# The p\*v matmuls of sliding-window attention, issued by key block first instead of by head half first, in a one-core hybrid encoder layer

## Chip, cores and metric

The kernel runs on one core of a Trainium2 chip. The metric is the device time of one execution in microseconds (us); for the kernel before, the median of three runs is 2016.85.

## What is computed

One layer of a streaming encoder, for 1024 frames of a new stream and 32 frames of a running one, model width 1024, all in float32. After a conditioning vector has scaled and shifted the input, one wide projection gives queries, keys and values of two branches and their gates. Branch A is sliding-window attention (16 query heads, 2 key/value heads, head width 64), branch B an mLSTM matrix memory; both are projected, gated, merged and normalised, and a convolutional feed-forward part follows. The change is in branch A alone. Its core in the reference:

```python
def banded_attention(qb, kb, vb, qpos, kpos, sinks):
    s = jnp.einsum('nbqhgd,nbshd->nbhgqs', qb.astype(jnp.float32), kb.astype(jnp.float32)) * (HEAD_DIM_A ** -0.5)
...
    s = s - slopes[None, None, :, :, None, None] * dist[None, :, None, None]
    s = jnp.where(visible[None, :, None, None], s, -jnp.inf)
...
    mx = jnp.maximum(jnp.max(s, -1, keepdims=True), sink)
    p = jnp.exp(s - mx)
    p = p / (jnp.sum(p, -1, keepdims=True) + jnp.exp(sink - mx))
    o = jnp.einsum('nbhgqs,nbshd->nbqhgd', p, vb.astype(jnp.float32))
    return o.astype(qb.dtype)
```

A chunk of 64 queries sees the keys of its own and the two chunks before, at most 192; the running stream's 32 queries see 128 cached keys and their own 32.

## The kernel before

Every engine has a program of its own, written out by hand, and semaphores tie them. Features lie on the partitions, positions on the free dimension. A weight panel (128 output columns of a projection) comes by DMA, POOL splits it into a high and a low part (L365, L367), and TensorE runs three matmuls for each of 8 input blocks and each third of the positions (gemm_half, L400): a whole panel is six "half panels" of 12 matmuls.

Attention runs interleaved with the panels of the other branch. For each of the 17 chunks (16 of the new stream, 1 of the running one) and each of the two key/value groups there is what is called a unit here, a = 2c + g, so 34 units, 0 to 33. On TensorE a unit goes through three steps with a half panel behind each, and the units overlap in a pipeline (att_chunk, L488): scores of unit a+1, half panel, transposes of unit a, half panel, p\*v of unit a, half panel.

- att_scores (L454): q times k for four head pairs into px banks 0 and 1, L463; for g = 0 also the transposes of v, L460 and L461.
- VectorE adds the ALiBi term and takes the maximum (att_max, L1247), ScalarE takes the exponential (att_exp, L834), VectorE normalises (att_norm, L1272, the product at L1278).
- att_transpose (L467): the probabilities are turned, block of older keys to bank 2 (L472), own chunk to bank 3 (L473); ScalarE copies them to pta (L844) and ptb (L845).
- att_values (L476): p\*v. The output is bank 4, partitions 0 to 63 for the even head of each pair (e = 0) and 64 to 127 for the odd one (e = 1), 256 columns (4 pairs of 64 queries). For each e, the first matmul takes the older keys (rows w - kb: 128 from chunk 2 on, 64 in chunk 1, none in chunk 0; L482), the second the own chunk (kb = 64 rows, 32 for the running stream; L484), accumulated. A weight operand is 64 columns of v, so an instruction fills 64 columns of the array.
- att_take (L1281, the copy at L1285): VectorE moves bank 4 to SBUF. It comes in VectorE's order between att_max and att_norm of the next unit.

The wait for pt_rdy and o_used stands ahead of the first p\*v matmul, the last one raises pv_rdy, for which att_take and the next copy to pta wait. VectorE has other work at two places of attention: behind chunk 3 it prepares rows of mLSTM gates (L1305 to L1311), behind chunk 15 it scans them (L1317 to L1323), each time before att_max of the next chunk.

Of the kernel before, what the change touches and what calls it, by code (L numbers as in the profile page):

```python
# [27 lines left out]
CH = 64  # L28
# [102 lines left out]
def wait(eng, sem, v):  # L131

    if isinstance(v, int) and v <= 0:
        return
    eng.wait_ge(sem, v)


def build(nc, io):
    ctx = ExitStack()
    with ctx:  # L140
# [18 lines left out]
        def after(name, shape, dt=F32):  # L159
            return at(name, shape, (place["end"] + 31) // 32 * 32, dt)  # L160
# [30 lines left out]
        vt = after("v_tok", [P, 2, 2, P])  # L191
        pb = after("probs", [P, 2, 4, BAND])
        pta = after("probs_ta", [P, 4, P])
        ptb = after("probs_tb", [P, 4, P])
# [56 lines left out]
        px = ctx.enter_context(nc.psum_tensor("px", [P, 5, 512], F32))  # L251
# [54 lines left out]
        def weights(p):  # L306
            return wo[:, p - WO_PANELS[0], :, :] if p in WO_PANELS else wt[:, p - TAIL_PANELS[0], :, :] if p in TAIL_PANELS else whl[:, SLOT[p], :, :]
# [81 lines left out]
        def _(pe):  # L389
            mm = nc.tensor.matmul  # L390
# [21 lines left out]
            for m in range(KT + 4):  # L412
                if 1 <= m <= KT:
                    pe.wait_ge(ada_row, m)
                    wait(pe, ada_mod, m - 1)
                    for i in range(2):
                        last = nc.tensor.transpose(px[:, 4, 2 * i:2 * i + 2], mrow[:, (m - 1) % 2, i * P:(i + 1) * P],
                                                   ident[0:2, 0:2])
                    last.then_inc(ada_col, 1)
                if m < KT:  # L420
                    for i in range(2):
                        q = 2 * m + i
                        pe.wait_ge(ada_in[q % KT], (q // KT + 1) * 16)
                        for k in range(KT):
                            last = mm(px[0:2, 3, i * P:(i + 1) * P], silu[:, 1, k, :], ada[:, q % KT, k * P:(k + 1) * P],  # L425
                                      start=(k == 0), stop=(k == KT - 1))
                        last.then_inc(ada_used, 1)
                for p in range(2):
# [7 lines left out]
                    for j, (wi, xi) in enumerate(((0, 0), (0, 1), (1, 0))):  # L436
                        for n in range(NT):
                            last = mm((acc, px)[p][:, n, 0:NW], whl[:, p, wi, k * P:(k + 1) * P],
                                      XA[:, xi, k, n * NW:(n + 1) * NW], start=(k == 0 and j == 0),
                                      stop=(k == KT - 1 and j == 2))  # L440
# [35 lines left out]
            def att_values(a, par, g, w, kb):  # L476
                pe.wait_ge(pt_rdy, a + 1)
                wait(pe, o_used, a)
                for e in range(2):
                    out = px[64 * e:64 * e + 64, 4, 0:4 * CH]  # L480
                    if w > kb:
                        mm(out, vt[0:w - kb, par, 0, g * 64:g * 64 + 64], pta[0:w - kb, :, 64 * e:64 * e + 64],  # L482
                           start=True, stop=False)
                    last = mm(out, vt[0:kb, par, 1, g * 64:g * 64 + 64], ptb[0:kb, :, 64 * e:64 * e + 64],  # L484
                              start=(w == kb), stop=True)
                last.then_inc(pv_rdy, 1)

            def att_chunk(c, par, w, kb, wp, kbp):  # L488

                slot = SLOT[P_ATT + c]  # L490
                first = isinstance(c, int) and c == 0
                for g in range(2):
                    if first and g == 0:
                        for half in range(2):
                            gemm_half(P_ATT, slot, 0, half, XA)
                        att_scores(0, 0, 0, 0, w, kb)
                        gemm_half(P_ATT, slot, 1, 0, XA)
                        continue
                    before = (c * 2 - 1, 1 - par, 1, wp, kbp) if g == 0 else (c * 2, par, 0, w, kb)
                    att_scores(c, c * 2 + g, par, g, w, kb)  # L500
                    gemm_half(c + P_ATT, slot, *divmod(3 * g, 2), XA)
                    att_transpose(before[0], before[2], before[3], before[4])
                    gemm_half(c + P_ATT, slot, *divmod(3 * g + 1, 2), XA)
                    att_values(*before)
                    gemm_half(c + P_ATT, slot, *divmod(3 * g + 2, 2), XA)
# [8 lines left out]
            att_chunk(NCH, 0, WIN + TS, TS, BAND, CH)  # L514
            att_transpose(2 * NCH + 1, 1, WIN + TS, TS)
            att_values(2 * NCH + 1, 0, 1, WIN + TS, TS)


# [8 lines left out]
            for h in range(HB):  # L527
                last = mm(px[:, 0, 128 + 9 * h:137 + 9 * h], sel[:, h, :], mprow[:, :], start=True, stop=True)
# [175 lines left out]
            w = weights(P_OUT)  # L704
            for k in range(KT):
                pe.wait_ge(mg_lo, k + 1)
                for j, (wi, xi) in enumerate(((0, 0), (0, 1), (1, 0))):
                    for n in range(NT):
                        last = mm(first[n], w[:, wi, k * P:(k + 1) * P], XA[:, xi, k, n * NW:(n + 1) * NW],
                                  start=(k == 0 and j == 0), stop=(k == KT - 1 and j == 2))  # L710
# [1017 lines left out]
```

## Time and profile before

| | |
|---|---|
| median of 3 runs | 2016.85 us (2012.32 to 2017.06) |
| profiled execution, its time | 2017.29 us |
| its span | 2015.5 us |
| TensorE busy (PE) | 1947.1 us, 97% |
| weight loads (PEld) | 1847.2 us, 92% |
| VectorE (DVE) / ScalarE (ACT) / POOL | 52% / 31% / 27% |
| mean granted clock of TensorE | 0.986 |

A row of the timeline has a start and a time in us from the start of the span, the engine, the line, the operation, "output<-inputs" and shapes. For a matmul "128\*64" is the part of the array in use, rows by columns, and "128x256" the moving operand; a float32 matmul instruction leaves two records, so "x2" is one instruction. Brackets at the end hold the engine's idle time before the row and what released it. Neighbouring records of one kind are merged into one row. How fast matmuls run is read from their starts, since a record's end is modelled and overlaps its neighbour.

### The profile page before, as it was taken

How to read it: one execution, taken by the hardware profiler on the slowest of the kernel's cores; microseconds unless marked ns; L12 is line 12 of the kernel's file. 1: busy time of each engine (PE TensorE's matmuls, PEld its weight loads, DVE VectorE, ACT ScalarE, POOL GpSimd, SP SyncE). 2: the span in 40 equal slices, each digit the busy share in tenths (PEclk: the TensorE clock that was granted, in tenths of full speed). 3: DMA queues.
4: the chain of work that ended last, by engine and by line, in shares of the span. 5: the costliest groups of instructions: out<-in, count | busy, mean ns of one | idle time of the engine just before them, and what ended most of it. 6: DMA issues, size and time to landing. Idle time of an engine off the chain costs nothing.

```text
span 2015.5 us, 29507 instructions
## 1 busy us (share of the span) xinstructions
PE 1947.1 (97%) x11919; PEld 1847.2 (92%) x11919; DVE 1045.8 (52%) x1885; ACT 621.3 (31%) x1409; POOL 553.4 (27%) x312
## 2 busy tenths in 40 slices
PE   8889999999999999999899999999999999999995
PEld 6889888888799999988899998999999999999995
DVE  2796454434543333454434487754454455535488
ACT  1102543445222232334311136322222223222333
POOL 2332212111122222212233624432323323233230
PEclk9999999999999999999999999999999999999997
DMA  7562111111222333324634300111111111111102
GB/s 309 200 200 97 66 43 59 48 43 64 76 85 96 109 124 99 115 69 163 206 105 158 112 20 2 62 53 43 42 53 43 53 42 43 53 43 52 43 30 79
DMA packets 74184, 171.40 MB, mean 85 GB/s; under 512 B 8496, under 2 KB 37680, under 8 KB 73920
## 3 DMA queue, kind: packets, MB, share of 16 engines
q1 hardware_dynamic: 27168, 91.50, 13.3%
q10 hardware_dynamic: 46880, 78.02, 11.6%
q8 instruction: 94, 1.54, 0.3%
q14 instruction: 42, 0.34, 0.1%
HBM read 137.27 MB, written 32.22 MB: 84 GB/s over the span
## 4 chain that ended last, share of the span: by engine, by line
PE 85%; DVE 9%; ACT 2%; DVEq 1%; issue 1%; ACTq 1%; DMA 1%; POOL 0%; POOLq 0%
PE acc L400 30%; PE px L670 15%; PE acc L670 9%; PE px L680 7%; PE acc L680 4%; DVE adaT_tmp L1222 4%; PE px L647 2%; PE px L463 2%; PE px L484 2%; PE px L482 2%; PE px L425 2%; PE acc L647 1%; PE px L564 1%; PE px L566 1%; PE px L565 1%
## 5 line engine op out<-in xcount | busy, mean ns | idle before, releaser
L400 PE MATMUL acc<-x_hilo_a,w_hilo 128*128 128x352 f32 x4176 | 730.7, 330 | 20.8 <-ACT x_c L780 9.9
L400 PEld LDWEIGHTS acc<-x_hilo_a,w_hilo 128*128 128x128 f32 x4176 | 677.5, 191 | 39.8 <-issue 29.1
L365 POOL CAST w_hilo<-w_raw 128x1024 fp32r<-128x1024 f32 x133 | 144.3, 1085 | 1296.5 <-PE acc L400 790.2
L367 POOL TENSOR_TENSOR w_hilo<-w_raw,w_hilo 128x1024 fp32r<-128x1024 f32 x133 | 342.3, 2574 | 10.6
L670 PE MATMUL px<-x_hilo_a,w_hilo 128*128 128x352 f32 x1968 | 319.2, 322 | 0.0
L670 PEld LDWEIGHTS px<-x_hilo_a,w_hilo 128*128 128x128 f32 x1968 | 315.4, 189 | 0.5 <-issue 0.5
L670 PE MATMUL acc<-x_hilo_a,w_hilo 128*128 128x352 f32 x1200 | 194.2, 321 | 0.0
L670 PEld LDWEIGHTS acc<-x_hilo_a,w_hilo 128*128 128x128 f32 x1200 | 191.4, 188 | 0.0
L680 PE MATMUL px<-ffn_act,w_hilo 128*128 128x352 f32 x864 | 146.2, 324 | 0.0
L680 PEld LDWEIGHTS px<-ffn_act,w_hilo 128*128 128x128 f32 x864 | 140.3, 189 | 0.2
L1100 ACT ACTIVATE u_rows<-px,ffn_consts 128x352 f32<-128x352 f32 (+2 forms) x110 | 49.5, 478 | 238.6 <-PE px L670 238.6
L1546 DVE SCALAR_TENSOR_TENSOR x_c<-px,mod,x_c 128x352 f32<-128x352 f32 (+2 forms) x181 | 80.4, 483 | 64.4 <-PE px L680 64.4
L1517 DVE COPY conv_out<-u_rows 128x2 f32<-128x2 f32 x44 | 17.3, 394 | 171.5 <-ACTq L1105 171.4
L1520 DVE SCALAR_TENSOR_TENSOR stage<-u_rows,ffn_consts,stage 128x1058 f32<-128x1058 f32 x44 | 88.9, 2021 | 21.5 <-ACT stage L1107 21.5
L1222 DVE CUSTOM_DVE_ANT_0 adaT_tmp<-adaT_ring,silu_bc 128x1024 f32<-128x1024 f32 x64 | 94.1, 1507 | 5.1 <-issue 4.2
L849 ACT ACTIVATE stage<-acc 128x352 f32<-128x352 f32 x123 | 54.9, 457 | 130.7 <-PE acc L400 114.1
L680 PE MATMUL acc<-ffn_act,w_hilo 128*128 128x352 f32 x504 | 87.6, 324 | 2.6 <-POOL w_hilo L367 1.5
L680 PEld LDWEIGHTS acc<-ffn_act,w_hilo 128*128 128x128 f32 x504 | 81.8, 189 | 3.3 <-issue 3.1
L1100 ACT ACTIVATE u_rows<-acc,ffn_consts 128x352 f32<-128x352 f32 (+2 forms) x66 | 30.2, 482 | 164.8 <-PE acc L670 164.8
L400 PE MATMUL acc<-x_hilo_b,w_hilo 128*128 128x352 f32 x504 | 80.5, 322 | 0.5 <-DVE stage L1439 0.5
L400 PEld LDWEIGHTS acc<-x_hilo_b,w_hilo 128*128 128x128 f32 x504 | 80.3, 188 | 0.7 <-issue 0.7
L1546 DVE SCALAR_TENSOR_TENSOR x_c<-acc,mod,x_c 128x352 f32<-128x352 f32 (+2 forms) x107 | 48.4, 487 | 56.8 <-PE acc L680 56.8
(231 smaller groups left out, 2318.9 us busy)
## 6 DMA issues: line engine op xcount, KB each, us to landing
w_raw<-in_w_panels SPq DMA_DIRECT2D x142, 512.0 KB, 3.7
z_spill<-stage ACTq DMA_DIRECT2D x41, 528.0 KB, 2.6
adaT_ring<-in_w_adaT ACTq DMA_DIRECT2D x32, 512.0 KB, 4.2
stage<-z_spill ACTq DMA_DIRECT2D x20, 528.0 KB, 4.8
ada_ring<-in_w_ada SPq DMA_DIRECT2D x16, 512.0 KB, 9.4
zc<-z_spill ACTq DMA_DIRECT2D x8, 1024.0 KB, 7.5
x_c<-in_x SPq DMA_DIRECT2D x8, 528.0 KB, 10.1
x_c<-in_x ACTq DMA_DIRECT2D x8, 528.0 KB, 3.8
```

What stands on the lines that cost most here:

```text
L365: nc.gpsimd.tensor_copy(to[:, 0, :], raw[:, s, :]).then_inc(w_hi, 1)
L367: nc.gpsimd.tensor_tensor(to[:, 1, :], raw[:, s, :], to[:, 0, :].bitcast(F32), ALU.subtract).then_inc(w_ready, 1)
L400: last = mm(acc[:, n, 0:NW], whl[:, slot, wi, k * P:(k + 1) * P], rhs[:, xi, k, n * NW:(n + 1) * NW], start=(k == 0 and j == 0), stop=(k = ...
L425: last = mm(px[0:2, 3, i * P:(i + 1) * P], silu[:, 1, k, :], ada[:, q % KT, k * P:(k + 1) * P], start=(k == 0), stop=(k == KT - 1))
L647: last = mm(to, w[:, wi, k * P:(k + 1) * P], XA[:, xi, k, n * NW:(n + 1) * NW], start=(k == 0 and j == 0), stop=(k == KT - 1 and j == 2))
L670: last = mm(to, w[:, wi, k * P:(k + 1) * P], XA[:, xi, k, n * NW:(n + 1) * NW], start=(k == 0 and q == 0), stop=(k == KT - 1 and q == 2))
L680: done = mm(to, w[:, wi, col:col + P], act[:, xi, k, n * NW:(n + 1) * NW], start=(first and k == 0 and q == 0), stop=(last and k == 1 and ...
L849: A(ST[:, slot, n * NW:(n + 1) * NW], acc[:, n, 0:NW], ACT.Copy).then_inc(acc_free[n], 1)
L1100: last = A(ub[:, i, 2 + a + 2 * s:2 + b + 2 * s], src[:, a - n * NW:b - n * NW], ACT.Identity, bias=fc[:, j, i, 0:1])
L1222: V.tensor_tensor_reduce(adaT_tmp[:, s, :], adaT[:, i, :], sbc[:, s, :], 1.0, 0.0, ALU.mult, ALU.add, ast[:, i, s:s + 1])
L1520: V.scalar_tensor_tensor(ST[:, i, 0:CW], ub[:, i, 0:CW], fc[:, j, i, 1:2], ST[:, i, 0:CW], ALU.mult, ALU.add)
L1546: last = V.scalar_tensor_tensor(XC[:, m, a:b], src[:, a - n * NW:b - n * NW], mod[:, 5, m, s:s + 1], XC[:, m, a:b], ALU.mult, ALU.add)
```

## The change

The loop over the two halves e is turned inside out: first the older-key block for both halves, then the own chunk for both. Each output half is accumulated as before, in the same order of its two terms. skip_group_check only tells the build that two accumulations are open at once. Nothing else is changed.

```diff
--- before.py
+++ after.py
@@ -476,13 +476,14 @@
             def att_values(a, par, g, w, kb):
                 pe.wait_ge(pt_rdy, a + 1)
                 wait(pe, o_used, a)
+                outs = [px[64 * e:64 * e + 64, 4, 0:4 * CH] for e in range(2)]
+                if w > kb:
+                    for e in range(2):
+                        mm(outs[e], vt[0:w - kb, par, 0, g * 64:g * 64 + 64], pta[0:w - kb, :, 64 * e:64 * e + 64],
+                           start=True, stop=False, skip_group_check=True)
                 for e in range(2):
-                    out = px[64 * e:64 * e + 64, 4, 0:4 * CH]
-                    if w > kb:
-                        mm(out, vt[0:w - kb, par, 0, g * 64:g * 64 + 64], pta[0:w - kb, :, 64 * e:64 * e + 64],
-                           start=True, stop=False)
-                    last = mm(out, vt[0:kb, par, 1, g * 64:g * 64 + 64], ptb[0:kb, :, 64 * e:64 * e + 64],
-                              start=(w == kb), stop=True)
+                    last = mm(outs[e], vt[0:kb, par, 1, g * 64:g * 64 + 64], ptb[0:kb, :, 64 * e:64 * e + 64],
+                              start=(w == kb), stop=True, skip_group_check=True)
                 last.then_inc(pv_rdy, 1)
 
             def att_chunk(c, par, w, kb, wp, kbp):
```

On TensorE the p\*v step of a unit with 128 older keys, with the neighbouring rows ("x2" here is two instructions that read alike; lines with - are those of before, with + those of the change; L400 is the half panel, L460 the first transpose of the next unit):

```order
 L400 MATMUL acc<-x_hilo_a,w_hilo 128x352 x11
 L482 MATMUL px<-probs_ta,v_tok 64x256 [waits o_used,pt_rdy]
-L484 MATMUL px<-probs_tb,v_tok 64x256
-L482 MATMUL px<-probs_ta,v_tok 64x256
-L484 MATMUL px<-probs_tb,v_tok 64x256
+L482 MATMUL px<-probs_ta,v_tok 64x256
+L485 MATMUL px<-probs_tb,v_tok 64x256 x2
 L400 MATMUL acc<-x_hilo_a,w_hilo 128x352 x12
 L460 MATMUL px<-ident,v_stage 128x128 [waits s_used,st_rdy]
```

The first instruction with its waits stays, the two L482 now stand together and the two own-chunk ones behind them.

The second place is behind chunk 15, TensorE's side in the changed kernel, from the half panel ahead of the p\*v of unit 31 to the scores of unit 33 (the last of the running stream's two):

```order
L400 MATMUL acc<-x_hilo_a,w_hilo 128x352 x12
L482 MATMUL px<-probs_ta,v_tok 64x256 [waits o_used,pt_rdy]
L482 MATMUL px<-probs_ta,v_tok 64x256
L485 MATMUL px<-probs_tb,v_tok 64x256 x2
L400 MATMUL acc<-x_hilo_a,w_hilo 128x352 [waits acc_free1]
L400 MATMUL acc<-x_hilo_a,w_hilo 128x352 x11
L463 MATMUL px<-k_stage,q_stage 128x160 [waits s_used]
L463 MATMUL px<-k_stage,q_stage 128x160 x3
```

Between this p\*v step and the scores that wait for s_used lies one half panel, as before; only the two middle p\*v matmuls have changed places.

The third is VectorE's side of the same place in the changed kernel, from the take of unit 30 to the first row of unit 32 (line numbers are one higher than before):

```order
L1286 COPY x_c<-px 128x4x64 [waits pv_rdy]
L1275 TENSOR_TENSOR row_den<-row_sum,exp_sink 128x4 [waits ex_rdy]
L1277 RECIPROCAL row_den<-row_den 128x4
L1279 TENSOR_TENSOR probs<-probs,row_den 128x768
L1318 TENSOR_TENSOR rowC<-rowC,rowD 4x1056 [waits row_a]
L1320 TENSOR_TENSOR stage<-stage,rowC 4x1056
L1322 SCALAR_TENSOR_TENSOR rowD<-rowE,stage 4x1056
L1323 SCALAR_TENSOR_TENSOR rowM<-stage 4x1024
L1324 SCALAR_TENSOR_TENSOR rowM<-stage,small 4x32
L1253 TENSOR_TENSOR probs<-px,alibi 128x2x160 [waits tr_rdy,s_rdy]
```

Nothing moved here. The gate rows stand between the normalising of unit 31 and the row that takes up the scores of unit 32.

## Rows read from the trace of the kernel before

**Rows 1.** page of the profile: span, TensorE's busy time, chain by line
```profile
span 2015.5 us, 29507 instructions
PE 1947.1 (97%) x11919; PEld 1847.2 (92%) x11919; DVE 1045.8 (52%) x1885; ACT 621.3 (31%) x1409; POOL 553.4 (27%) x312
PE acc L400 30%; PE px L670 15%; PE acc L670 9%; PE px L680 7%; PE acc L680 4%; DVE adaT_tmp L1222 4%; PE px L647 2%; PE px L463 2%; PE px L484 2%; PE px L482 2%; PE px L425 2%; PE acc L647 1%; PE px L564 1%; PE px L566 1%; PE px L565 1%
```
**Rows 2.** windows, the attention stretch: busy by engine, PEclk, DMA share, GB/s
```profile
190.00:560.00 370.00, 365.18 (x2156) 307.06 (x2155) 161.86 (x396) 158.12 (x509) 64.75 (x36) 1.00 0.16 57
```
**Rows 3.** waits of TensorE, 190 to 700: in total, times, longest
```profile
PE px L472 <- DVE probs L1278: 1.6, 1, 1.6
PE px L463 <- DVEq L1260: 0.7, 1, 0.7
```
**Rows 4.** timeline, V(10) on TensorE: start us, us, engine line operation
```profile
300.23 0.65 PE L482 MATMUL px<-probs_ta,v_tok 128*64 128x256 f32 x2
300.81 0.64 PE L484 MATMUL px<-probs_tb,v_tok 64*64 64x256 f32 x2
301.38 0.65 PE L482 MATMUL px<-probs_ta,v_tok 128*64 128x256 f32 x2
302.53 0.43 PE L400 MATMUL acc<-x_hilo_a,w_hilo 128*128 128x352 f32 x1
```
**Rows 5.** groups by line and form, L482: busy us, mean ns
```profile
L482 PE MATMUL px<-probs_ta,v_tok 128*64 128x256 f32 x120 | 38.7, 405 | 1.3 <-ACT probs_tb L845 1.3
L482 PE MATMUL px<-probs_ta,v_tok 64*64 64x256 f32 x8 | 1.3, 402 | 0.0
```
**Rows 6.** timeline, V(0) in chunk 0, matmuls and weight loads
```profile
202.02 0.65 PE L484 MATMUL px<-probs_tb,v_tok 64*64 64x256 f32 x4
202.02 0.20 PEld L484 LDWEIGHTS px<-probs_tb,v_tok 64*64 64x64 f32 x4 [0.22 <-issue]
202.60 0.43 PE L400 MATMUL acc<-x_hilo_a,w_hilo 128*128 128x352 f32 x1
```
**Rows 7.** timeline, V(2) in chunk 1, TensorE
```profile
218.42 0.66 PE L482 MATMUL px<-probs_ta,v_tok 64*64 64x256 f32 x4
219.44 0.43 PE L400 MATMUL acc<-x_hilo_a,w_hilo 128*128 128x352 f32 x1
```
**Rows 8.** timeline, unit 11: normalise, transpose, copy, p*v
```profile
303.45 0.96 DVE L1278 TENSOR_TENSOR probs<-probs,row_den 128x768 f32<-128x768 f32 x1
308.01 0.27 PE L472 MATMUL px<-ident,probs 128*128 128x128 f32 x1
309.58 0.58 ACT L845 ACTIVATE probs_tb<-px 64x512 f32<-64x512 f32 x1
310.90 0.65 PE L482 MATMUL px<-probs_ta,v_tok 128*64 128x256 f32 x2
```
**Rows 9.** timeline, behind chunk 3: take, normalise of unit 8, its transposes
```profile
260.43 0.42 DVE L1285 COPY x_c<-px 128x256 f32<-128x256 f32 x1 [4.20 <-PE px L484]
274.84 0.96 DVE L1278 TENSOR_TENSOR probs<-probs,row_den 128x768 f32<-128x768 f32 x1
276.25 0.27 PE L472 MATMUL px<-ident,probs 128*128 128x128 f32 x1
```
**Rows 10.** timeline, behind chunk 15: take, scan, scores and transposes that wait
```profile
513.63 0.42 DVE L1285 COPY x_c<-px 128x256 f32<-128x256 f32 x1 [3.84 <-PE px L484]
518.84 4.39 DVE L1321 TENSOR_TENSOR_SCAN rowD<-rowE,stage 4x1056 f32<-4x1056 f32 x1
526.84 1.35 PE L463 MATMUL px<-k_stage,q_stage 128*128 128x160 f32 x8 [0.68 <-DVEq L1260]
531.70 0.33 PE L472 MATMUL px<-ident,probs 128*128 128x128 f32 x1 [1.60 <-DVE probs L1278]
```
**Rows 11.** windows, two stretches at the end of attention (columns of rows 2)
```profile
540.00:543.40 3.40, 2.14 (x8) 0.75 (x8) 1.72 (x1) 1.06 (x2) 3.32 (x2) 1.00 0.41 164
543.40:547.00 3.60, 3.60 (x14) 3.38 (x13) 1.43 (x6) 0.00 (x0) 0.52 (x1) 0.53 0.52 151
```

## Prediction

> **What bounds the kernel now.** I read the page first. TensorE is busy for 97% of the span and the chain that ended last is nearly all TensorE, the p\*v lines L482 and L484 with 2% each in it [rows 1]. A busy TensorE can still contain time in which it streams nothing, so the share alone does not say what an edit of its work is worth; I went on to the attention stretch. There, of 370 us, TensorE is busy for 365.18 at full granted clock, while VectorE and ScalarE are busy for less than half [rows 2]. The waits of TensorE in and after it are single ones, the longest of a kind 1.6 us [rows 3]. So what attention takes is what TensorE's own instructions take one after another, and time cut there comes off the end, as long as nothing else is late.
>
> Then the timeline of one p\*v step. I call a chunk and key/value group a unit (34 of them, 0 to 33, two to a chunk) and its rows between two half panels V(a). V(10) starts at 300.23 and the half panel behind it at 302.53 [rows 4]: 2.30 us for four matmul instructions, each of them two passes in the trace ("x2"). The four start 0.57 to 0.58 us apart. Every neighbour has another height: 128\*64, 64\*64, 128\*64, 64\*64. The boundary at 300.81 keeps the column half and the one at 301.38 changes it too, and both cost the same, so the half change beside a height change is free.
>
> The chunks at the start are the test of what these gaps are. In chunk 0 there is one key block, so V(0) is two 64\*64 instructions, one for each column half. Both together take from 202.02 to 202.60, 0.58 us, as long as one instruction of V(10); all four passes stand in one row of 0.65 us, and all four weight loads lie within 0.20 us from 202.02 [rows 6]. The halves ran at the same time. In chunk 1 the first block has 64 rows too, so V(2) is four 64\*64 instructions in the old order, and it takes 218.42 to 219.44, 1.02 us in place of 2.30 [rows 7]. The array thus overlaps the two halves by itself wherever the neighbours have one height, and works off an instruction at a time where the height changes.
>
> **The change part by part.** It issues the same instructions with the same shapes and waits. It only swaps the middle two of four, so the heights run 128, 128, 64, 64 (32 in the last chunk) and the halves 0, 1, 0, 1. The first instruction still carries the wait on both semaphores and the last still raises pv_rdy.
>
> *Units 0 and 1* have one block and two instructions: unchanged, 0. *Units 2 and 3* have one height in either order and overlap already [rows 7]: 0.
>
> *Units 4 to 33*: the trace has 120 passes of the 128\*64 form [rows 5], four to a unit, so 30 units. A unit becomes two pairs, each of equal height on alternate halves. The nearest row for a pair is V(0), 0.58 us [rows 6]; it differs in that only 64 of the rows of the array are used. For the 64- and 32-row pair it is nearly the same case. For the 128-row pair the trace shows nothing, and the bounds are 0.58 (full overlap) and 1.15 (two instructions at 0.575 as in [rows 4]). I take 0.58, because a 128\*64 and a 64\*64 instruction by themselves take equal time in [rows 4], so height costs nothing in any row. A unit then takes 2 x 0.58 = 1.16, against 2.30: **1.14 us less**. 30 x 1.14 = 34.2 us.
>
> A written rule speaks against the pair. [Rows 6] have the four loads packed into 0.20 us, beside matmuls that started at 202.02 in the same 64 rows of the array. The Trainium skill ("TensorE: Matmul & The Clock Gate", Part 3, packing small matmuls) says that a weight load overlaps a matmul in flight only where its row group is another one; two halves of the same rows would then not overlap and the sum would be zero. The trace disagrees with it for 64 rows, and for 128 rows no row here decides; its case is rival B.
>
> *What hides nothing and what is late next.* After V(a) comes a half panel, then scores, half panel, transposes. VectorE waits for the end of V(a), takes the result and normalises the next unit, which starts from the end of V(a) and so moves with it. For unit 11 the normalised probabilities end at 303.45 + 0.96 = 304.41 and their transposes start at 308.01: 3.60 us of room, which the change leaves as it is, since only the time inside V shrinks. The copy of the transposed block ends at 309.58 + 0.58 = 310.16, and V(11) starts at 310.90: 0.74 us of room, with no V in between, so it stays too [rows 8]. A unit goes from about 10.5 to 9.4 us; ScalarE and VectorE, at 158 and 162 of 370 us [rows 2], can follow. POOL, which splits one panel in two units, is busy for 65 of the 370 us, and the transfers take a share of 0.16 [rows 2]: neither is near its limit at 10% more pace.
>
> Two places hold other VectorE work (the mLSTM's gate rows), where this does not hold.
> - Behind chunk 3: from the take at 260.43, released by V(6), VectorE runs gate rows, the maximum and the softmax of unit 8 up to 274.84 + 0.96 = 275.80; the transposes start at 276.25 [rows 9]. Room 0.45. TensorE meanwhile passes V(7), which is 1.14 shorter, and VectorE's stretch is not: 1.14 - 0.45 = 0.69 is lost again.
> - Behind chunk 15: from the take at 513.63, released by V(30), the scans and the maximum of unit 32 run until the scores of unit 33, which already waited 0.68 us [rows 10]. V(31) lies in between, so its whole 1.14 turns into a longer wait (to about 1.8 us). The wait of 1.60 at 531.70 hangs on the same VectorE stretch and stays.
>
> Sum: 34.2 - 0.69 - 1.14 = **32.4 us less**. Everything behind attention is as long as before and starts earlier. The profiled execution took 2017.29 us (span 2015.5, and 1.8 around it), so it would take 1984.9. The median of the runs shown is 0.44 lower, 2016.85: **1984.5 us**, 1.6% less.
>
> Of the clock: it went to half for one stretch of about 3.4 us at the end of attention, granted 0.53 in the window from 543.4 and 1.00 before it, right behind a window of 3.4 us in which TensorE was busy for 2.14 [rows 11]. Such a stretch costs some 1.7 us (half of 3.4). The longer wait near 525 may bring one, and the shorter V(33) may spare the one at 543. I count neither, and put both into the range.
>
> **The rivals.**
> *A, the 128-row pair does not overlap but is not held up by its height either.* The second instruction of a column, at equal height, costs 1.02 - 0.58 = 0.44 us more [rows 6, 7]. If the halves only queue, a pair takes 0.58 + 0.44 = 1.02, a unit 2.04 and the gain is 30 x 0.26 less the one lost at V(31), 7.5 us: 2009.3 us. If this holds for the 128-row pair alone, a unit takes 1.02 + 0.58 = 1.60 and the gain is 30 x 0.70 less 0.95, about 20 us: 1996.8. For it: no row shows two halves at 128 rows. Against: in [rows 4] height had no price. Chance 0.07, both forms together.
>
> *B, nothing overlaps and each instruction still takes its 0.575*, because the second half's load waits until the first half's matmul has ended. Unit 2.30 as before, 2016.9 us. For it the 0.57 at each of the four starts in [rows 4]; against it [rows 6]. Chance 0.03. The same time would come out if the build kept the old order; the rows of the order above show that it doesn't.
>
> *C, slower.* The three inner boundaries of a unit were two height changes and one of height and half. They become two half changes and one of both. If a half change at 128 rows costs more than a height change, say by the 0.22 us for which the load side stood idle ahead of V(0) [rows 6], then 2 x 0.22 x 30 = 13.2 us come on: 2030.1 us. It decides from the point at which a half change costs more than 0.575 us from start to start. Against: V(0) has a half change by itself and hides it altogether [rows 6], and 301.38 has one at no price [rows 4]. Chance 0.02.
>
> *D, a wait takes the place of part of the gain everywhere.* The softmax of unit a+1 must be ready when V(a) has been taken. If ScalarE were late by up to 0.5 us in each unit, the transposes would still have 3 us of room [rows 8]. So this stays inside the forecast and has no chance of its own.
>
> **How the numbers follow.** Forecast 0.88, A 0.07, B 0.03, C 0.02. The forecast's own range: without the two losses 1.8 less, with the clock's stretch spared 1.7 less, 1981; with two more such stretches 3.4 more, 1988. One us is added at either end for the scatter of the runs (the lowest of three was 4.5 below the median): **1980 to 1989**. The other cases are 0.12 together and lie outside; that leaves about 0.8 inside. What a measurement of this kernel can tell from no change is about 0.3%, 6 us; faster by more than that are the forecast and A, 0.95; within it B, 0.03; slower C, 0.02.
>
> **What would show it.** In the changed kernel's timeline a V step of a unit from 4 on should be 1.16 us long, with two rows of four passes ("x4"), one of L482 and one of L485. V(2) should still be 1.02 and V(0) 0.58. The stretch from the first scores to the last V should be about 32 us shorter. The scores of unit 33 should wait about 1.8 us for VectorE, and the transposes of unit 8 about 0.7. The step on the pair is wrong if the 128\*64 row and the 64\*64 row of a unit lie 1.0 us or more apart. The step on hidden work is wrong if V is 1.16 but TensorE shows new waits in the middle chunks.

## The result and the profile after

The changed kernel takes 1982.76 us (median of 4 runs, 1982.71 to 1983.44) against 2014.98 us (median of 4, 2012.32 to 2017.06): a ratio of 0.9844, 95% interval 0.9832 to 0.9856. The forecast was 1984.5 us in a range of 1980 to 1989. The profiled execution took 1982.71 us, 34.6 us less than the profiled one before. Its page:

```profile
span 1980.9 us, 29507 instructions
...
PE 1911.2 (96%) x11919; PEld 1834.3 (93%) x11919; DVE 1042.5 (53%) x1885; ACT 621.3 (31%) x1409; POOL 554.2 (28%) x312
...
PE acc L400 30%; PE px L671 16%; PE acc L671 10%; PE px L681 8%; PE acc L681 5%; DVE adaT_tmp L1223 4%; PE px L648 2%; PE px L463 2%; PE px L425 2%; PE acc L648 1%; PE px L485 1%; PE px L482 1%; PE px L565 1%; PE px L567 1%; PE px L566 1%
```

As many instructions, TensorE 36 us less busy, and the p\*v lines in the chain fell from 2% each to 1% [rows 1]. TensorE still bounds the kernel.

V(10) in the timeline of the changed kernel, matmuls first, then the weight loads (columns as in [rows 4]):

```profile
293.67 0.65 PE L482 MATMUL px<-probs_ta,v_tok 128*64 128x256 f32 x4
294.26 0.65 PE L485 MATMUL px<-probs_tb,v_tok 64*64 64x256 f32 x4
294.83 0.43 PE L400 MATMUL acc<-x_hilo_a,w_hilo 128*128 128x352 f32 x1
```

```profile
293.67 0.20 PEld L482 LDWEIGHTS px<-probs_ta,v_tok 128*64 128x64 f32 x4 [0.22 <-issue]
294.25 0.19 PEld L485 LDWEIGHTS px<-probs_tb,v_tok 64*64 64x64 f32 x4 [0.39 <-issue]
```

Where there were four starts 0.575 us apart, there are two 0.58 apart, each with four passes in one row of 0.65 us. The step goes from 293.67 to 294.83, 1.16 us, as forecast. The two 128-row instructions run together just as the two 64-row ones of V(0) did, with their four loads packed into 0.20 us.

Two waits of TensorE, 190 to 700 us of the changed kernel (total, times, longest), and in the timeline the one that is new (0.60) and the one that has grown (1.87, from 0.68 before [rows 10]):

```profile
PE px L472 <- DVE probs L1279: 2.2, 2, 1.6
PE px L463 <- DVEq L1261: 1.9, 1, 1.9
```

```profile
271.91 0.33 PE L472 MATMUL px<-ident,probs 128*128 128x128 f32 x1 [0.60 <-DVE probs L1279]
496.43 0.40 PE L463 MATMUL px<-k_stage,q_stage 128*128 128x160 f32 x1 [1.87 <-DVEq L1261]
```

These are the transposes of unit 8, behind chunk 3, and the scores of unit 33, behind chunk 15. Between 276 and 490 us, in the middle chunks, nothing waits.

From the first scores to V(33) the changed kernel takes 509.73 - 192.2 = 317.6 us; before it was 541.26 - 192.5 = 348.8. That is 31.2 us, and with the 1.14 inside V(33) itself 32.4, the sum of the forecast. The first scores and V(33), before (from the source line's summary, whose first and last starts stand behind the comma, and the timeline), then after:

```profile
L463 PE MATMUL px<-k_stage,q_stage x272: 217/326/403, 192.5 to 527.9; 128*128 128x192 f32 x112, 128*128 128x64 f32 x8, 128*128 128x128 f32 x8, 128*128 128x160 f32 x8
541.26 0.43 PE L482 MATMUL px<-probs_ta,v_tok 128*64 128x256 f32 x1 [1.28 <-ACT probs_tb L845]
```

```profile
L463 PE MATMUL px<-k_stage,q_stage x272: 217/326/404, 192.2 to 497.5; 128*128 128x192 f32 x112, 128*128 128x64 f32 x8, 128*128 128x128 f32 x8, 128*128 128x160 f32 x8
509.73 0.65 PE L482 MATMUL px<-probs_ta,v_tok 128*64 128x256 f32 x4 [1.28 <-ACT probs_tb L846]
```

That this meets the forecast to the tenth is partly luck. TensorE also waits ahead of V(0), for VectorE at unit 0's transposes, by an amount that differs between runs with the same TensorE work ahead of it: 1.26 and 1.21 us in the two profiles of the kernel before, 1.03 and 1.05 in those of the changed one, 0.84 to 1.40 in the other versions. The wait before, then after:

```profile
199.55 0.63 PE L473 MATMUL px<-ident,probs 128*64 128x128 f32 x4 [1.26 <-DVE probs L1278]
```

```profile
199.01 0.63 PE L473 MATMUL px<-ident,probs 128*64 128x128 f32 x4 [1.03 <-DVE probs L1279]
```

From V(0) to V(33) it is 339.24 before (202.02 to 541.26) and 308.24 after (201.49 to 509.73): 31.0 us, with V(33) 32.1. The missing 0.3 lies mostly in the two losses: around unit 8 the starts of V(7) and V(8) are 10.11 us apart (below), those of V(9) and V(10) 9.29 (284.38 and 293.67), so 0.82 is lost where 0.69 was forecast, and V(31) to V(32) grew from 12.96 to 13.01 although V(31) is 1.14 shorter, so 1.19 is lost where 1.14 was forecast. The starts of V(7) and V(8):

```profile
264.74 0.65 PE L482 MATMUL px<-probs_ta,v_tok 128*64 128x256 f32 x4
274.85 0.65 PE L482 MATMUL px<-probs_ta,v_tok 128*64 128x256 f32 x4
```

The 2.2 us by which the two profiled executions differ beyond 32.4 are outside of the attention steps, most of them right behind: from the start of V(33) to the first of the gate rows' transposes (552.93 before, 518.72 after) it is 2.68 us less, 1.54 more than V(33) itself gave, because of a stretch of half clock (below).

### The profile page after: what moved, and what is told of

It is laid out like the page before. It is cut to its first block, busy times and chain, and to the rows that moved or that the text cites. A ratio compares the mean times of both kernels' runs of the same rounds, so it can differ in the third digit from the quotient of the medians.

```text
span 1980.9 us, 29507 instructions
## 1 busy us (share of the span) xinstructions
PE 1911.2 (96%) x11919; PEld 1834.3 (93%) x11919; DVE 1042.5 (53%) x1885; ACT 621.3 (31%) x1409; POOL 554.2 (28%) x312
## 3 DMA queue, kind: packets, MB, share of 16 engines
q8 instruction: 94, 1.54, 0.3%
## 4 chain that ended last, share of the span: by engine, by line
PE 84%; DVE 9%; ACT 2%; DVEq 2%; issue 1%; ACTq 1%; DMA 1%; POOL 0%; POOLq 0%
PE acc L400 30%; PE px L671 16%; PE acc L671 10%; PE px L681 8%; PE acc L681 5%; DVE adaT_tmp L1223 4%; PE px L648 2%; PE px L463 2%; PE px L425 2%; PE acc L648 1%; PE px L485 1%; PE px L482 1%; PE px L565 1%; PE px L567 1%; PE px L566 1%
## 5 line engine op out<-in xcount | busy, mean ns | idle before, releaser
L400 PE MATMUL acc<-x_hilo_a,w_hilo 128*128 128x352 f32 x4176 | 729.1, 330 | 21.1 <-ACT x_c L781 10.1
L400 PEld LDWEIGHTS acc<-x_hilo_a,w_hilo 128*128 128x128 f32 x4176 | 675.9, 190 | 40.0 <-issue 29.3
L400 PE MATMUL acc<-x_hilo_b,w_hilo 128*128 128x352 f32 x504 | 80.4, 321 | 0.5 <-DVE stage L1440 0.5
L400 PEld LDWEIGHTS acc<-x_hilo_b,w_hilo 128*128 128x128 f32 x504 | 80.1, 188 | 0.7 <-issue 0.7
```

Source lines behind the costliest of these rows:

```text
L400: last = mm(acc[:, n, 0:NW], whl[:, slot, wi, k * P:(k + 1) * P], rhs[:, xi, k, n * NW:(n + 1) * NW], start=(k == 0 and j == 0), stop=(k = ...
```

## The experiments

I call the stretch from the first scores to the start of V(33) the *attention section* (348.8 before, 317.6 after). It is read off each trace in the same way, and says more than a total, since totals of one kernel lie up to 10 us apart (2010.39 to 2019.98 in 7 runs of the kernel before). It still contains the wait ahead of V(0); the distance from V(0) to V(33) doesn't, and is the steadier of the two:

| | first scores to V(33) | V(0) to V(33) |
|---|---|---|
| before, and again (9) | 348.77, 348.75 | 339.24, 339.27 |
| changed, and again (10) | 317.56, 317.59 | 308.24, 308.26 |
| 1, old order, one height | 314.86 | 305.75 |
| 2, new order, one height | 313.92 | 304.25 |
| 3, both on one half | 343.02 | 333.88 |
| 4, halves 0, 1, 1, 0 | 317.46 | 308.26 |
| 5, only unit 33 new | 348.77 | 339.26 |
| 6, all new but unit 33 | 317.90 | 308.23 |
| 7, gate rows spread | 314.51 | 304.91 |
| 8, one height and spread | 310.13 | 300.82 |

### 1. The old order at one height

Is it the order or the height that decides? The order is left as it was; the operands of the own chunk get 64 rows of zeros in units 4 to 31 (the last chunk keeps its 32 rows).

```diff
+                kr = P if w == BAND else kb
                 for e in range(2):
...
-                    last = mm(out, vt[0:kb, par, 1, g * 64:g * 64 + 64], ptb[0:kb, :, 64 * e:64 * e + 64],
+                    last = mm(out, vt[0:kr, par, 1, g * 64:g * 64 + 64], ptb[0:kr, :, 64 * e:64 * e + 64],
...
             V.memset(qs[:, :, :, :], 0.0)
+            V.memset(vt[CH:P, :, 1, :], 0.0)
+            V.memset(ptb[CH:P, :, :], 0.0)
```

> The kernel before, in its old order (both blocks of half 0, then of half 1), but the own-chunk operands of units 4 to 31 are filled up with zeros to 128 rows, so that all four matmuls of a V step have one height. Theory H (a change of height between neighbours makes TensorE finish the one before it starts the next; at equal height the halves run together): V of these 28 units falls from 2.30 to about 1.02 us, as V(2) did; 28 x 1.28 = 35.8 us, less 1.28 lost at V(31) and 0.83 at V(7): about 33.7 us less than the kernel before, near 1981. Rival O (what counts is that neighbours lie in different halves, the height doesn't matter): the old order keeps V at 2.30 and the time at that of the kernel before, about 2015.

Measured: 1980.03 us (median of 4; ratio to before 0.983, 0.9808 to 0.9853). The attention section is 314.9 us, 33.9 less than before. V(10) in its timeline:

```profile
290.51 0.66 PE L483 MATMUL px<-probs_ta,v_tok 128*64 128x256 f32 x4
290.99 0.61 PE L485 MATMUL px<-probs_tb,v_tok 128*64 128x256 f32 x4
291.53 0.43 PE L400 MATMUL acc<-x_hilo_a,w_hilo 128*128 128x352 f32 x1
```

The step takes 1.02 us. The old order is *faster* than the new one once the height is one. All four passes of L483, those of half 1 too, stand ahead of those of L485, though in the program both blocks of half 0 come first: the second half's first matmul did not wait for its turn. Rival O falls. What the old order had against it was the height change at each of its inner boundaries, and the new order brings three of them down to one.

### 2. The new order at one height

The same zero rows on the changed kernel; the two memsets of experiment 1 belong to the edit too.

```diff
+                kr = P if w == BAND else kb
...
-                    last = mm(outs[e], vt[0:kb, par, 1, g * 64:g * 64 + 64], ptb[0:kb, :, 64 * e:64 * e + 64],
+                    last = mm(outs[e], vt[0:kr, par, 1, g * 64:g * 64 + 64], ptb[0:kr, :, 64 * e:64 * e + 64],
```

> The changed kernel with the same zero rows in units 4 to 31: new order and one height. H: V about 1.02 in place of 1.16, since one more height change is gone; 28 x 0.14 less 0.28 in the two covered places, about 3.6 us less than the changed kernel, near 1979, and the same as the old order with one height. O: nothing left to gain, V stays at 1.16 and the time at 1983.

Measured: 1976.44 us (median of 4; ratio to before 0.9816, 0.9795 to 0.9836), attention section 313.9 us, 3.6 less than the changed kernel as expected (4.0 less from V(0) on). V(10) again 1.02 us:

```profile
291.08 0.65 PE L482 MATMUL px<-probs_ta,v_tok 128*64 128x256 f32 x4
291.56 0.60 PE L486 MATMUL px<-probs_tb,v_tok 128*64 128x256 f32 x4
292.10 0.43 PE L400 MATMUL acc<-x_hilo_a,w_hilo 128*128 128x352 f32 x1
```

So a last height change costs 0.14 us (second rows start 0.48 behind the first in place of 0.58, and the end follows), and 64 rows of zeros cost TensorE nothing. From V(0) on it is 1.5 us shorter than experiment 1, which had old-order steps in the two units of the last chunk, whose own block has 32 rows: V(32) is 1.1 us longer there. The rest is about 0.01 us in each unit.

### 3. Both heads on one half

The overlap by itself: heights as in the changed kernel, but no second half. The odd heads' products go to columns 256 to 511 of the bank, which nobody reads, so their attention output is left out.

```diff
-                outs = [px[64 * e:64 * e + 64, 4, 0:4 * CH] for e in range(2)]
+                outs = [px[0:64, 4, 4 * CH * e:4 * CH * e + 4 * CH] for e in range(2)]
...
+            V.memset(px[64:P, 4, 0:4 * CH], 0.0)
```

> The changed kernel, but both heads' outputs go to partitions 0 to 63 (columns 0 to 255 and 256 to 511 of the bank), so all p*v matmuls lie in one column half; the odd heads' attention output is left out. Heights run as in the changed kernel. H: a pair of equal height queues on one half, 0.58 + 0.44 = 1.02, V = 2.04, so 30 x 0.88 more, less 0.88 at V(31) and 0.69 at V(7): about 25 us over the changed kernel, near 2008. Rival (fewer height changes are all of it, the half is of no account): V stays at 1.16, 1983.

Measured: 2008.09 us (one run), attention section 343.0 us, 25.5 more than the changed kernel (25.6 from V(0) on).

```profile
297.65 1.08 PE L482 MATMUL px<-probs_ta,v_tok 128*64 128x256 f32 x4
298.65 1.07 PE L485 MATMUL px<-probs_tb,v_tok 64*64 64x256 f32 x4
299.66 0.43 PE L400 MATMUL acc<-x_hilo_a,w_hilo 128*128 128x352 f32 x1
```

A pair on one half takes 1.00 us, a step 2.01. This divides the gain of a unit: of 1.14 us, 0.29 come from the height changes and 0.85 from the halves running together. Neither alone is the change's effect. The division is the one in this order: no version overlaps with a height change at every boundary. The expectation left units 0 to 3 out; they grow as well, V(0) from 0.58 to 1.00 and V(2) from 1.01 to 1.87, with one height throughout. In return the wait at unit 8 is gone.

### 4. Halves in the order 0, 1, 1, 0

```diff
-                for e in range(2):
+                for e in (1, 0):
                     last = mm(outs[e], vt[0:kb, par, 1, g * 64:g * 64 + 64], ptb[0:kb, :, 64 * e:64 * e + 64],
```

> The changed kernel with the second pair in the other order: halves 0, 1, 1, 0. The boundary in the middle of a V step changes the height alone and keeps the half. H: V stays at 1.16 and the time at about 1983 (within 1 us). Rival (neighbours in different halves count at each boundary, as the change is described): the middle boundary costs more, V above 1.16, at most 0.44 more in each of 30 units, up to 13 us.

Measured: 1979.41 us (one run), attention section 317.5 us, as in the changed kernel.

```profile
291.94 0.65 PE L482 MATMUL px<-probs_ta,v_tok 128*64 128x256 f32 x4
292.52 0.65 PE L485 MATMUL px<-probs_tb,v_tok 64*64 64x256 f32 x4
293.10 0.43 PE L400 MATMUL acc<-x_hilo_a,w_hilo 128*128 128x352 f32 x1
```

V(10) is 1.16 us. That neighbours alternate between the halves is not what matters at the boundary in the middle. The total is 3.3 us below the changed kernel's with the same steps; it differs in its clock (mean granted 0.989 against 0.987; experiments 5, 6, 9 and 10).

### 5 and 6. Unit 33 alone new, and all but unit 33 new

Both put the two versions of the step behind a test of the unit:

```diff
+                if a == 2 * NCH + 1:
...
+                else:
```

(a != 2 * NCH + 1 in the second.) They were made for the stretch of half clock behind V(33) [rows 11], which the profile of the changed kernel doesn't have.

> The kernel before with the new order in unit 33 alone, the last of attention. The profile before had a stretch of half clock right behind V(33) (3.4 us long), the profile after has none there. Theory C (the stretch comes of the thin TensorE work around V(33), and the shorter V removes it): granted clock 1.00 behind V(33), 1.14 us from V and about 1.7 us from the clock less. Rival (it comes or stays by where the whole program lies in time): the stretch stays, 1.14 us less only.

> The changed kernel with the old order in unit 33 alone. C: the stretch of half clock behind V(33) is back, about 1.14 + 1.7 = 2.8 us over the changed kernel. Rival: no stretch, 1.1 us over it.

Measured: 2013.23 and 1986.21 us (one run each). Windows around the end of V(33), PEclk is the third number from the end; first experiment 5, then 6, then the changed kernel:

```profile
542.00:546.00 4.00, 4.00 (x17) 4.00 (x16) 1.25 (x6) 0.00 (x0) 1.23 (x1) 0.57 0.54 149
```

```profile
512.00:516.00 4.00, 4.00 (x15) 3.40 (x15) 1.43 (x6) 0.00 (x0) 0.88 (x1) 0.57 0.52 149
```

```profile
510.50:514.50 4.00, 4.00 (x27) 3.62 (x25) 1.43 (x6) 0.00 (x0) 1.93 (x1) 1.00 0.37 77
```

Experiment 6 looks like theory C (the stretch is back, 3.5 us over the changed kernel where 2.8 was expected), experiment 5 speaks against it: V(33) is short there (1.16 us), and the stretch stands. Two single executions don't settle it, so the two kernels were profiled once more.

### 9 and 10. The two kernels once more

> The kernel before, unchanged, profiled once more for its clock. If the stretch of half clock behind V(33) belongs to the kernel, it is there again, near 543 us. If it is a matter of the single execution, the list of stretches differs from that of the first profile in place or length, with the same instruction times between them.

> The changed kernel, unchanged, profiled once more for its clock. If its freedom from a stretch near the end of attention belongs to the kernel, there is none again between 480 and 530 us; if it is a matter of the execution, one may stand there, as with the halves in the order 0, 1, 1, 0. V steps of 1.16 us, the waits of 0.6 and 1.9 us and the 32.4 us between the first scores and the last V step must be the same in either case.

Measured: 2013.22 and 1982.78 us. The attention sections are 348.8 and 317.6 us, as the first time; in the repeated changed kernel the waits near 272 and 496 us are there again. The kernel before again, the windows that answer to [rows 11]:

```profile
539.00:542.60 3.60, 2.32 (x9) 0.76 (x8) 1.73 (x1) 1.06 (x2) 3.52 (x2) 1.00 0.38 155
542.60:546.00 3.40, 3.40 (x22) 3.40 (x22) 1.43 (x6) 0.00 (x0) 0.34 (x1) 1.00 0.54 162
```

The same thin window ahead, and this time no stretch of half clock behind it: so it belongs to the execution and not to the kernel. It isn't the only difference. Around 930, 990 and 1227 us both executions have stretches, but of double length in the first; one of the three, first execution, then second:

```profile
1224.00:1234.00 10.00, 6.89 (x22) 5.53 (x23) 6.23 (x10) 4.15 (x10) 2.06 (x2) 0.66 0.00 0
```

```profile
1224.00:1234.00 10.00, 9.14 (x46) 8.67 (x47) 7.28 (x9) 2.52 (x8) 0.33 (x1) 0.83 0.00 0
```

That is 4.1 us between two executions of one kernel (2017.29 and 2013.22). The changed kernel had the same list of stretches both times, and experiment 4, with its instruction times, one that holds less half clock in all, though it has a stretch at 494 us where the changed kernel has none. That one cost nothing:

```profile
494.69 2.47 PE L463 MATMUL px<-k_stage,q_stage 128*128 128x160 f32 x8 [1.86 <-DVEq L1261]
```

The scores of unit 33 took 2.47 us there in place of 1.35, but the 1.57 us that the transposes of unit 32 wait for VectorE right behind them in the changed kernel are gone, and V(32) starts 13.01 us after V(31) in both. What picks the list was not found.

### 7. The gate rows spread

The gain that was lost at V(7) and V(31) was put down to VectorE's gate rows. Here they are moved between chunks, with nothing left out.

```diff
+            att_chunk(4, 0, BAND, BAND)
             V.tensor_scalar(rowI, rowI, small[0:HB, C_BI:C_BI + 1], None, ALU.add)
-            dve.drain()
+            att_chunk(5, 1, BAND, BAND)
             V.tensor_scalar(rowR[:, :], rowD[:, :], -1.0, None, ALU.add).then_inc(row_d, 1)
...
-            for i in range(2, NCH // 2):
+            for i in range(3, NCH // 2 - 1):
...
+            att_chunk(NCH - 2, 0, BAND, BAND)
             dve.wait_ge(row_a, 2)
...
+            att_chunk(NCH - 1, 1, BAND, BAND)
             dve.drain()
             V.tensor_tensor_scan(rowD[:, :], rowE[:, :], rowF, 0.0, ALU.mult, ALU.add)
```

> The changed kernel, VectorE's gate rows spread: of the five behind chunk 3 one goes behind chunk 4 and two behind chunk 5, and the two row operations ahead of the scans go from behind chunk 15 to behind chunk 14. If the gain lost at V(7) and V(31) hangs on these rows as the prediction says, the wait of the transposes of unit 8 (0.6 us) and of the scores of unit 33 (1.9 us) go, and the 1.6 us at the transposes of unit 32 shrinks: 2.5 to 4 us less than the changed kernel, near 1979 to 1980. Rival (VectorE's stretch is bound by something else, the softmax on ScalarE or the semaphores): less than 1 us.

Measured: 1977.68 us (median of 4, 1974.44 to 1980.02; ratio to before 0.9811, 0.9793 to 0.9829), attention section 314.5 us, 3.0 less than the changed kernel. Waits of TensorE, 190 to 600:

```profile
PE px L473 <- DVE probs L1279: 1.3, 1, 1.3
PE px L482 <- ACT probs_tb L846: 1.3, 1, 1.3
PE px L472 <- DVE probs L1279: 1.2, 1, 1.2
```

The wait of the scores of unit 33 (1.9) is gone, and so is the one at unit 8 (the 1.2 left on L472 is unit 32's, 1.6 before). The rows were the cause. The total fell by 5.1 us, 2 more than the section; the mean granted clock of the profiled execution was 0.990 against 0.987, and I put the rest down to it.

### 8. One height and spread rows together

The edits of experiments 2 and 7 on the changed kernel.

> New order, zero rows in units 4 to 31 and spread gate rows together. If both gains stand on different waits they add up: 28 x 0.14 = 3.9 (nothing lost at V(7) and V(31) now) and 2.5 to 4 us, near 1975 to 1976.5. If the one uses up the room of the other, near 1979.

Measured: 1973.56 us (median of 5, 1970.36 to 1975.48), ratio to the kernel before 0.979, 0.9772 to 0.9808. The attention section is 310.1 us, 7.4 less than in the changed kernel. From V(0) on it is 7.4 as well, and there the two parts by themselves gave 4.0 and 3.3: they add up. By the section they gave 3.6 and 3.0, since unit 0's transposes waited longer in both (1.40 and 1.32 us, 1.03 here and in the changed kernel). V(10):

```profile
292.26 0.65 PE L482 MATMUL px<-probs_ta,v_tok 128*64 128x256 f32 x4
292.74 0.60 PE L486 MATMUL px<-probs_tb,v_tok 128*64 128x256 f32 x4
293.27 0.43 PE L400 MATMUL acc<-x_hilo_a,w_hilo 128*128 128x352 f32 x1
```

It is the fastest version of this study. The totals of experiments 2, 7 and 8 all lie below what was expected of them (1976.44 for about 1979, 1977.68 for 1979 to 1980, 1973.56 for 1975 to 1976.5), while what attention gained was as expected; the clock is again the likely reason, not a shown one.

## Why the prediction was right

- *What bounds.* Right: TensorE's own time, cut by 32.1 us from V(0) to the end of V(33), came off the end (32.2 us between the medians), and outside the two named places the profile shows no new wait, so case D did not arise.
- *The pair.* 0.58 us for the 128-row pair was taken from a 64-row one, between bounds of 0.58 and 1.15. Measured 0.58 (293.67 to 294.26), and the step 1.16. Rivals A, B and C with it fell: A's queueing pair was real where both are on one half (experiment 3, 1.00 against the 1.02 that it priced), and there alone.
- *The cause.* That the gaps hang on the height was argued from [rows 4, 6, 7]; experiment 1 shows it without a change of order, experiment 4 shows that the half has no say at a boundary where the height changes, and experiment 3 that the halves' overlap is 0.85 of the 1.14 us. That neighbours lie in different halves is only what the new order looks like. What the overlap needs is neighbours of equal height, and work for both halves among them.
- *The rule weighed against the trace.* The rule of the Trainium skill ("TensorE: Matmul & The Clock Gate", Part 3) that loads overlap a matmul in flight only where the row group is another one, the base of rival B, is contradicted at 128 rows as well: four loads of one row group within 0.20 us from 293.67, beside matmuls that began then.
- *Units 2 and 3* kept their 1.02 us and units 0 and 1 their 0.58, as forecast.
- *Lost again.* Forecast 0.69 at unit 8 and a wait of about 1.8 us at unit 33; measured waits 0.60 and 1.87, and by the starts of the steps 0.82 and 1.19 were lost, together 0.2 more than forecast. Experiment 7 shows that the gate rows caused them.
- *The clock.* The one weak step. The text tied the stretch of half clock to the thin work around V(33) and the longer wait near 525, and guessed that the change may spare the one and bring the other. The repeated profile of the kernel before has none of it with the same work. The size (1.7 us for such a stretch) and the width it gave the range were of use, the mechanism was not. The totals' agreement within 1.8 us with the forecast leans on executions with unlike lists of stretches: the first pair of profiles differs by 34.6 us, the repeated pair by 30.4. The 31.0 us from V(0) to V(33) are the same in both pairs. The price was not general either: the stretch at 494 us in experiment 4 fell into a wait and cost nothing.

## What to carry to other kernels

A matmul that uses part of the array is priced by its neighbours. Look at the starts in the timeline, not at the busy share: in this kernel, where the used rows changed from one p\*v matmul to the next, the next began 0.58 us later, and two column halves ran at once only between such boundaries. So group small matmuls by height, or fill the lower ones up with zero rows, which here cost TensorE nothing and beat the reordering. And a kernel's short first chunks can be a ready-made experiment for the form that a change will give to the long ones.

## What was not expected of the hardware

- The order in the program does not have to be that of the starts: with one height, half 1's first block started before half 0's second, though issued behind it (experiment 1, and V(2) of the kernel before).
- Two executions of one kernel with the same instruction times differed by 4.1 us (2017.29 and 2013.22) by the number and length of stretches of half clock. Differences of a few us between two kernels are better read off a section. Choose its ends with care: from V(0) to V(33) the four versions with the changed kernel's steps agree within 0.03 us, from the first scores, with one wait more, only within 0.44.
